# Turning gathered rows on VectorE in blocks of 32, with four quarter-row gathers a step

## The reference

```python
s = jax.nn.sigmoid((t @ w_router[l]).astype(jnp.float32))
_, sel = lax.top_k(s + b_router[l].astype(jnp.float32), TOP_K)      # 8 of 64 experts a token
...
out = (jax.nn.silu(t @ w_s_gate[l]) * (t @ w_s_up[l])) @ w_s_down[l]    # the shared expert
for e0 in range(0, N_EXPERTS, EXPERT_GROUP):
    a = jnp.einsum('nd,edf->nef', t, w_e_gate[l, es])
    u = jnp.einsum('nd,edf->nef', t, w_e_up[l, es])
    hid = jax.nn.silu(a) * u * gates[:, es, None]
    out = out + jnp.einsum('nef,efd->nd', hid, w_e_down[l, es])
```

## Time and profile before

| | us |
|---|---|
| median of three runs (lowest, highest) | 1190.78 (1189.35, 1201.41) |
| profiled execution | 1198.63 |
| its span, first to last instruction | 1196.7 |
| PE busy in the span | 1070.6 (89%) |
| POOL busy in the span | 358.0 (30%) |
| DVE busy, ACT busy | 498.0 (42%), 367.6 (31%) |

### The profile page before, as it was taken

One profiled execution on the slowest core, in us unless ns is written; L12 is line 12 of the kernel. 1 busy time (PEld: TensorE's weight loads), 2 busy tenths in 40 slices (PEclk: granted clock), 3 DMA queues, 4 the chain that ended last, 5 costly groups with the idle time before them and its releaser, 6 DMA issues.

```text
span 1196.7 us, 24457 instructions
## 1 busy us (share of the span) xinstructions
PE 1070.6 (89%) x9716; PEld 644.8 (54%) x9716; DVE 498.0 (42%) x1249; ACT 367.6 (31%) x898; POOL 358.0 (30%) x411
## 2 busy tenths in 40 slices
PE   4899998899789966999999989999989899998596
PEld 2698895567764533455455545454545454554232
DVE  5437880264045577245416533332323232222146
ACT  4533432244244477311132222222222222222111
POOL 2233333323411243301023524343434343343100
PEclk9999998999899987899799989999989899999899
DMA  9322226654161000301375969797877879675596
GB/s 361 136 88 75 89 75 225 210 178 168 56 251 60 2 1 1 97 37 51 136 270 172 390 217 354 285 342 295 320 290 275 310 248 373 217 288 198 181 395 265
DMA packets 58417, 238.83 MB, mean 200 GB/s; under 512 B 22670, under 2 KB 22750, under 8 KB 46270
## 3 DMA queue, kind: packets, MB, share of 16 engines
q1 hardware_dynamic: 27792, 181.20, 41.0%
q0 software_dynamic: 30512, 56.06, 13.3%
HBM read 292.05 MB, written 47.40 MB: 284 GB/s over the span
## 4 chain that ended last, share of the span: by engine, by line
PE 74%; DMA 14%; ACT 4%; DVE 3%; issue 3%; POOL 2%; SPq 0%; DVEq 0%; POOLq 0%; ACTq 0%
PE bank L2061 16%; PE bank L2079 10%; DMA x_got<-x_dram,idx_tok 8%; PE bank L2043 5%; PE bank L1546 5%; PE bank L1548 4%; PE bank L1547 4%; PE bank L1869 4%; PE bank L2121 3%; PE bank L1574 3%; PE bank L1652 2%; PE bank L1963 2%; DMA w_stage<-in_w_in 1%; PE bank L1797 1%; DMA w_stage<-in_w_ada 1%
## 5 line engine op out<-in xcount | busy, mean ns | idle before, releaser
L2061 PE MATMUL bank<-slot,xt 128*32 128x256 f32 x4608 | 263.7, 381 | 6.9 <-issue 4.2
L2061 PEld LDWEIGHTS bank<-slot,xt 128*32 128x32 f32 x4608 | 151.3, 111 | 137.2 <-issue 50.3
L2079 PE MATMUL bank<-slot,hid_t 128*32 128x512 f32 x1152 | 144.6, 621 | 0.7 <-ACT hid_t L1511 0.7
L1546 PE MATMUL bank<-h_hi,w_hi 128*128 128x288 f32 x464 | 140.6, 303 | 0.0
L1547 PE MATMUL bank<-h_lo,w_hi 128*128 128x288 f32 x464 | 137.8, 297 | 0.0
L1548 PE MATMUL bank<-h_hi,w_lo 128*128 128x288 f32 x464 | 137.5, 296 | 0.0
L1505 ACT ACTIVATE sg<-bank 128x128 f32<-128x128 f32 x72 | 20.0, 277 | 279.8 <-PE bank L2061 279.8
L777 POOL TENSOR_TENSOR w_lo<-w_stage,w_hi 128x1024 fp32r<-128x1024 f32 x28 | 67.1, 2395 | 104.9 <-ACT w_hi L1242 104.8
L2043 PE MATMUL bank<-ident,x_got 128*128 128x128 f32 x576 | 78.8, 282 | 20.9 <-DMA x_got<-x_dram,idx_tok 20.9
L2564 DVE TENSOR_TENSOR hid<-sg,bank 128x128 f32<-128x128 f32 x72 | 20.7, 287 | 183.3 <-ACT sg L1505 175.1
L1546 PEld LDWEIGHTS bank<-h_hi,w_hi 128*128 128x128 f32 x464 | 88.2, 190 | 11.8 <-issue 11.4
(11 more groups left out here) (397 smaller groups left out, 1508.4 us busy)
## 6 DMA issues: line engine op xcount, KB each, us to landing
slot<-in_w_moe SPq DMA_DIRECT2D x65, 1536.0 KB, 9.1
w_stage<-in_w_ada SPq DMA_DIRECT2D x32, 512.0 KB, 5.1
pairs<-pair_dram SPq DMA_DIRECT2D x16, 1024.0 KB, 10.1
w_stage<-in_w_in SPq DMA_DIRECT2D x29, 512.0 KB, 3.7
resid<-in_w_ada SPq DMA_DIRECT2D x2, 2048.0 KB, 13.3
w_out_sb<-in_w_out SPq DMA_DIRECT2D x1, 4096.0 KB, 14.1
o_t<-in_x_t SPq DMA_DIRECT2D x4, 576.0 KB, 5.7
feat<-in_w_ada SPq DMA_DIRECT2D x1, 2048.0 KB, 18.6
```

The source lines that it names most:

```text
L1546: mm(out, hi_w, hi_x, start=first, stop=False)
L2061: ins = mm(bank[2 + i % 2][r, 0:2 * P], xt[:, i % 2, k, r], slot_of(place_no)[:, 2 * P * k:2 * P * (k + 1)], start=(k == 0), stop=(k == KD ...
L2079: ins = mm(bank[4 + 2 * (i % 2) + c][r, :], hid_t[:, i % 2, r], slot_of(place_no)[:, 2 * D + 512 * c:2 * D + 512 * c + 512], start=True, s ...
```

## The change

- TensorE no longer turns the rows. VectorE turns them straight from `x_got` to `xt` with one instruction a step, in blocks of 32 x 32 (`turn_x`, after the two waits on the gather and on the older `xt` buffer). The PSUM copies `x_half` on ScalarE and VectorE go.
- Blocks of 32 can't move data from one group of 32 partitions to another. So group q of partitions now holds quarter q of the features, for all four units: a step has four gathers of 128 quarter rows (1 KB each) out of `x_dram` seen as 2304 rows, one for each unit b, into columns 256 b to 256 b + 255. The routed experts' gate and up weights are laid out to match on the host.
- `idx_tok` has four columns a step, with 4 x token + quarter; `turn_lists` turns each list four times to all columns; `indices` has eight instructions where it had two.
- POOL gathers for step i + 4 in round i, where it gathered for i + 3. At the start it does gather(0), gather(1), the three first over loads, gather(2), gather(3), where it did the four gathers first.
- TensorE's order is gate_up(i), down(i - 1), turn_hidden(i). VectorE's is turn_x(i + 1), hidden(i), out_half(i - 1).

```diff
+        quarter_rows = x_dram.rearrange("t (a c) -> (t a) c", a=4)
...
             def gather(i):
+
                 if i >= 4:
-                    pool.wait_ge(x_turned, 2 * (i - 3))
+                    pool.wait_ge(xt_ready, i - 3)
                 pool.wait_ge(idx_ready, 1 + 4 * i // P)
-                g.indirect_dma_start(x_got[:, i % 4, :], None, x_dram,
-                                     bass.IndirectOffsetOnAxis(ap=idx_tok[:, i:i + 1], axis=0),
-                                     bounds_check=NT - 1, oob_is_err=False).then_inc(x_got_in[i % 4], 16)
+                for b in range(4):
+                    g.indirect_dma_start(x_got[:, i % 4, 256 * b:256 * b + 256], None, quarter_rows,
+                                         bass.IndirectOffsetOnAxis(ap=idx_tok[:, 4 * i + b:4 * i + b + 1], axis=0),
+                                         bounds_check=4 * NT - 1, oob_is_err=False).then_inc(x_got_in[i % 4], 16)
...
-            for i in range(4):
-                gather(i)
+            gather(0)
+            gather(1)
             pool.wait_ge(idx_w_ready, 1)
             for n in over_places:
                 if SLOT_FOR[n][2] is None:
                     load_over(n)
+            gather(2)
+            gather(3)
             for i in range(1, N_STEPS + 1):
-                if i + 3 < N_STEPS:
-                    gather(i + 3)
+
+                for n in ((4, 5) if i == 1 else (i + 4,)):
+                    if n < N_STEPS:
+                        gather(n)
...
             for i in range(N_STEPS):
                 gate_up(i)
                 if i:
-                    turn_hidden(i - 1)
-                if i + 1 < N_STEPS:
-                    turn_x(i + 1)
-                if i:
                     down(i - 1)
-            turn_hidden(N_STEPS - 1)
+                turn_hidden(i)
             down(N_STEPS - 1)
...
+                t = idx_tok[:, 4 * a:4 * (a + n)]
+                chain(v.tensor_scalar(t, src[:, 0:4 * n], -1.0, float(PAIR_END), ALU.mult, ALU.add))
+                for b in range(4):
+                    r = slice(PART * b, PART * b + PART)
+                    ins = v.tensor_copy(idx_pair[r, a:a + n], idx_tok[r, 4 * a + b:4 * (a + n):4])
+                chain(ins)
+                chain(v.tensor_scalar(t, t, 3, 2, ALU.logical_shift_right, ALU.logical_shift_left))
+                v.tensor_tensor(t, t, quarter[:, 0:1].broadcast_to([P, 4 * n]), ALU.bitwise_or).then_inc(idx_ready, 1)
...
-            def x_half(i):
-                dve.wait_ge(x_turned, 2 * i + 2)
+            def turn_x(i):
+                dve.wait_ge(x_got_in[i % 4], 64 * (i // 4 + 1))
                 if i >= 2:
                     dve.wait_ge(gu_full, i - 1)
-                v.tensor_copy(xt[:, i % 2, 4:8, :], bank[1][:, :].rearrange("p (k c) -> p k c", k=4)).then_inc(xt_dve, 1)
+                v.transpose(xt[:, i % 2, :, :].rearrange("p k (s c) -> p s k c", s=4),
+                            x_got[:, i % 4, :].rearrange("p (s k c) -> p s k c", s=4, k=KD)).then_inc(xt_ready, 1)
```

More of the change, by code:

```diff
@@ L523, in build @@
         idx_pair = at("idx_pair", [P, N_STEPS], after("unit_first"), U32)
-        idx_tok = at("idx_tok", [P, N_STEPS], after("idx_pair"), U32)
-        idx_w = at("idx_w", [P, N_UNITS], after("idx_tok"), U32)
+        idx_tok = at("idx_tok", [P, N_UNITS], after("idx_pair"), U32)
+        quarter = at("quarter", [P, 1], after("idx_tok"), U32)
+        idx_w = at("idx_w", [P, N_UNITS], after("quarter"), U32)
         unit_rank = at("unit_rank", [N_EXPERTS, N_UNITS], places["xt"][0])
@@ L602, in build @@
         x_got_in = [sem(f"x_got_in{i}") for i in range(4)]
-        x_turned, xt_act, xt_dve = sem("x_turned"), sem("xt_act"), sem("xt_dve")
+        xt_ready = sem("xt_ready")
         gu_full, sg_ready, hid_ready = sem("gu_full"), sem("sg_ready"), sem("hid_ready")
@@ L1135, in _ @@
             made(g.iota(row_end[:, :], pattern=[[0, 1]], base=N_NO_ROW, channel_multiplier=1, **iota))
+            made(g.iota(quarter[:, :], pattern=[[0, 1]], base=0, channel_multiplier=1))
             made(g.memset(ones[:, :], 1.0))
@@ L1938, in turn_lists @@
             def turn_lists(i, out):
-                a, n = LIST_TILES[i]
+                n = LIST_TILES[i][1]
                 pe.wait_ge(listed, i + 1)
                 for b in range(4):
-                    ins = mm(out[PART * b:PART * b + PART, 0:n // 4], lists[0:n, i, :], ident[0:n, b:n:4], start=True,
+                    ins = mm(out[PART * b:PART * b + PART, 0:n], lists[0:n, i, :], ident[0:n, 0:n], start=True,
                              stop=True, skip_group_check=True)
@@ L2012, in _ @@
             shared_prompt(1, 3, 5)
-            turn_lists(0, bank[3][:, 96:96 + PART])
+            pe.wait_ge(idx_w_ready, 1)
+            turn_lists(0, bank[3][:, 192:192 + P])
             shared_prompt(1, 5, KD)
@@ L2034, in _ @@
                        start=True, stop=True).then_inc(sd_full, 1)
-            def turn_x(i):
-                pe.wait_ge(x_got_in[i % 4], 16 * (i // 4 + 1))
-                if i:
-                    pe.wait_ge(xt_act, i)
-                    pe.wait_ge(xt_dve, i)
-                for k in range(KD):
-                    ins = nc.tensor.transpose(bank[k // 4][:, P * (k % 4):P * (k % 4) + P], x_got[:, i % 4, P * k:P * k + P],
-                                              ident[:, :])
-                    if k % 4 == 3:
-                        ins.then_inc(x_turned, 1)
             def gate_up(i):
@@ L2050, in gate_up @@
                     pe.wait_ge(ht_ready, i - 1)
-                    turn_lists(TURN_AT.index(i), bank[2 + i % 2][:, 3 * P:3 * P + PART])
+                    turn_lists(TURN_AT.index(i), bank[2 + i % 2][:, 3 * P:4 * P])
                 for place_no in sorted(set(places_of(i))):
                     wait_weights(pe, place_no)
-                pe.wait_ge(xt_act, i + 1)
-                pe.wait_ge(xt_dve, i + 1)
+                pe.wait_ge(xt_ready, i + 1)
                 if i >= 2:
@@ L2539, in indices @@
                 dve.wait_ge(lists_turned, i + 1)
-                chain(v.tensor_scalar(idx_pair[:, a:a + n], src[:, 0:n], -1.0, float(PAIR_END), ALU.mult, ALU.add))
-                v.tensor_scalar(idx_tok[:, a:a + n], idx_pair[:, a:a + n], 3, None, ALU.logical_shift_right)\
-                    .then_inc(idx_ready, 1)
+                t = idx_tok[:, 4 * a:4 * (a + n)]
[6 more added lines that the diff above has]
+                v.tensor_tensor(t, t, quarter[:, 0:1].broadcast_to([P, 4 * n]), ALU.bitwise_or).then_inc(idx_ready, 1)
+            chain(v.tensor_scalar(quarter[:, :], quarter[:, :], 5, None, ALU.logical_shift_right))
             find_units(0)
@@ L2547, in _ @@
             find_units(1)
-            indices(0, bank[3][:, 96:96 + PART])
+            indices(0, bank[3][:, 192:192 + P])
             find_units(2)
@@ L2665 @@
     down = np.concatenate([inputs["w_s_down"], inputs["w_e_down"][0]])
-    gate_up = np.stack([gate, up], axis=3).transpose(0, 2, 1, 3, 4).reshape(1 + N_EXPERTS, P, 2 * D)
+    both = np.stack([gate, up], axis=3)
+    gate_up = both.transpose(0, 2, 1, 3, 4).reshape(1 + N_EXPERTS, P, 2 * D)
+    by_quarter = both[1:].reshape(N_EXPERTS, 4, KD, PART, 2 * F).transpose(0, 1, 3, 2, 4)
+    gate_up = np.concatenate([gate_up[:1], by_quarter.reshape(N_EXPERTS, P, 2 * D)])
     laid_out = {k: v for k, v in inputs.items() if not k.startswith(("w_e_", "w_s_", "w_ada", "w_in", "c_", "subln"))}
```

23 lines of the change are left out of this document (6 added, 17 removed).

## The result

| | before | after |
|---|---|---|
| median of the runs timed together, us | 1194.39 | 1232.1 |
| lowest, highest, us | 1189.35, 1201.41 | 1227.26, 1236.75 |
| profiled execution; its span, us | 1198.63; 1196.7 | 1236.75; 1235.0 |
| third over load to last scatter, us | 507.75 | 543.2 |

The changed kernel is slower: ratio 1.035, 95% interval 1.030 to 1.040. The forecast was 1221 us, in a range of 1160 to 1270.

A forecast was written before the change was run, and what follows sets the result against it. POOL, with 7.39 us of indirect DMAs a step, replaces TensorE as the bound. The last scatter comes 22 us later, plus 5 for VectorE's holds: 27 us on 1198.63 or 1190.78, so 1221 us, range 1160 to 1270.

The forecast's parts named there:

- The bound moves to POOL: In the loop, POOL's indirect DMAs take 7.39 us a step, more than TensorE's 5.47 and the old mean of 7.05.
- the first rival: On POOL, quarter gathers without a wait issue without the 0.30 us gap: 63 us less, 1158 us; chance 0.17.
- the signs: In the loop: gathers 1.30 us apart, POOL busy about 77%, TensorE 410 to 450 us, its longest waits for VectorE's transpose.
- The sum: On POOL, from third over load to end of gather(71): gathers 365.4, scatters 86.5, over loads 58.1, together 510.0 us.
- holds by VectorE's sums: In steps 2 to 6, two-input VectorE sums hold up POOL: 1 us a pair, 5 us in all (0 to 9).
- I find no standing wait: In the loop, POOL never waits: scatter(i - 1) is issued some 29 us after gather(i), and its results need about 17.
- The tail: Behind gather(71), landing, turning and the last step up to the last scatter, with a little queueing: 20 us.
- The base: The profiled 1198.63 us lies 7.9 above the median: 1226 if those are loop stalls, 1218 if ahead of the loop.
- The small terms: VectorE's transpose of 1.25 us a step and index instructions delaying the first gather 1.1 to 1.6 us cost nothing.
- The gain on offer: On TensorE, removing the eight transposes saves 0.97 us a step, 72 x 0.97 = 70 us.
- Late landing: Rival: in the loop, small-row gathers land later than about 20 us allow; 1 us in 50 steps gives 1271; chance 0.04.
- The clock: Rival about the clock in the loop, where TensorE will idle 1.9 us a step; chance 0.02.

## Why the prediction was right, by its own steps

**The bound moves to POOL: right, and shown.** The four gathers alone bring the kernel before to 1234 us, fewer gathers bring the changed kernel under 1174, and neither bytes nor weights nor a second transpose move it by more than these runs can tell. The spacing of 1.30 us holds without any wait, so the gap is not the price of a wait, and the first rival falls. Of the signs, POOL's share (74% for 77%) and TensorE's work (438.34 us for 410 to 450) came as forecast. One failed: TensorE's longest waits were to be for VectorE's transpose, and they end with over loads. The sum has no term for that, since POOL's pace hangs little on it.

**The sum.** From the third over load to the end of gather(71) it had 510.0 us; it took 1142.62 - 621.22 = 521.4. The counts were right, 280 gathers, 66 scatters and 45 over loads. With their gaps these took 368.2, 88.4 and 58.3 us, 4.9 over the sum, of which 2.3 are holds by VectorE's sums. The step "I find no standing wait" was mis-sized: four scatters waited 1.1 to 2.2 us for results, 5.6 us beyond the usual gap, behind stops of gate_up. The last 0.9 us are gaps of 0.31 and small waits. The tail took 21.8 us for the 20 that I took, and holds had been put at 5 more. In all 543.2 for 535.0, 8 us.

**The base.** I left open whether the 7.9 us between the profiled execution and the median lie in the loop, and took a value in between. This stays open. The third over load moves by up to 13 us from trace to trace, and nearly all of that lies ahead of the product with `w_out_sb`. But in the trace of the kernel before it comes early, at 618.40, where only one of the other thirteen has it earlier, so nothing shows the 7.9 us there. What is shown is that the median of three was low: with more executions it is 1194.4 to 1198.7, and 1232.1 less the 35.4 of the loop is 1196.7. Of the 11 us by which 1221 was short, some 8 are the loop's and the rest is the base.

**The small terms.** The transpose takes 1.24 us (1.25 taken). The new index instructions put the first gather 1.26 us further behind the lists (1.1 to 1.6 expected), and the third over load covered it: it still waited 3.00 us for the shared expert. VectorE's sums held POOL, but for 2.3 us in all rather than 5: five of its rows were lengthened, by 0.1 to 0.94 us. The longest, with the sum beside it:

```profile
670.81 1.21 DVE L2568 TENSOR_TENSOR sh_rows<-sh_rows,gf_bc 128x1024 f32<-128x1024 f32 x1
670.96 1.94 POOL L1179 DMA_INDIRECT x_got<-x_dram,idx_tok  x1 [0.30 <-DVE squares L2561]
```

All rows of POOL above 1.06 us in the loop lie beside these sums, none beside a transpose alone. Beside a sum, which reads two inputs in SBUF, a row took up to 1.94 us; the rows that overlap a transpose, which reads one, took 1.01 us in the mean and 1.06 at most, with 72 transposes and with 144. That the number of inputs makes the difference is not shown: the two differ in the operation as well.

**The gain on offer was wrong.** "72 x 0.97 = 70 us. This is the whole gain on offer" held for TensorE's instructions and not for the time. The step fell by 0.88 us, 63 us in all, since 0.09 of the 0.97 came back between the other products; and with POOL out of the way only 27 of them show, since over loads that land late in the weights' bursts hold TensorE next. The time of the first rival, 1158 us, rested on it and would hardly have come: the kernel with one gather, which leaves POOL more room than that rival does, ended at 1171. The mean DMA share of 0.76 that I read in the earlier trace rows hid stretches of 1.0. The forecast didn't rest on this, since POOL's 7.39 us lay above either pace.

**Late landing** is not it either: half the bytes, or lighter weights, leave the time where it was. VectorE's transpose waited 40.0 us for gathers, but it still waits 41.2 us with half the bytes and 51.5 with lighter weights, so the bytes don't make the gathers late; that POOL's pace does is my reading of it.

**The clock** dipped (0.89 in the loop for 0.97) and cost little: gate_up took up to 6.56 us behind a stop, but TensorE caught up in steps of 5.56, and of POOL's 521.4 us only 5.6 are waits for results. No run shows a loop at a low clock throughout, for which the 0.02 stood: in windows of 10 us the changed kernel's lowest was 0.50 (680 to 690), around the end of a stop of 8.10 us, and the next window was at 1.00.

## What to carry to other kernels

Before work is moved off the bounding engine, count what the move adds to the engine that issues the indirect DMAs: here one of 128 rows costs 1.30 us whatever its bytes (512 bytes to 12 KB a row), so one gather may become two but not four. Read the mean DMA share window by window before a gain is called on offer; the next bound stood in its bursts. Where an engine's stop is put down to issue, look up which of its inputs landed last: here it was an over load, and not the gather that the change was about. And an engine's late input that disappears under an edit may only have been the first of several inputs that the same burst makes late.

## What the runs showed of the hardware

An indirect DMA cost POOL about 0.90 us and 0.9 ns for each row (estimated from 955 ns with 64 rows and 1013 with 128), and 0.30 us until the next one could start, with or without a wait; pieces of 512 bytes and of 1, 2, 4 and 12 KB cost the same within a few per cent (0.99 to 1.03 us), gathered or scattered. A 12 KB-a-row load of this kind landed anywhere between 2.1 and 21.5 us after its issue (the latter with two gathers); with one gather the six that ended the long stops took 18.4 to 20.7 us, and the windows of 10 us ahead of them had a DMA share of 1.00 to 1.03. VectorE turned 128 x 1024 float32 in 32 x 32 blocks in 1.24 us, the time of a sum of that size (1.225); POOL's gathers kept their 1.013 us in the mean beside it. In windows of 10 us with a DMA share of 1.00 or more, loads, gathers and scatters together moved 351 to 424 GB/s with one gather.
